# Recurrent stage: where the preparation of the next unit stands on PE, ACT and DVE

## The chip, the cores and the metric

The kernel runs on one core of a Trainium2 chip, as one program with a queue of instructions for each engine: PE (matrix products), ACT (activations and copies), DVE (elementwise work), POOL and SP. The metric is the time of one execution on the device, in microseconds (us), and lower is better.

## What is computed

Two transformer layers run after each other. The change touches one stage of the second: the bidirectional RWKV-7 scan of `rwkv7_time_mix`, cut here to its core (512 tokens, 8 heads of 64, both directions).

```python
w_raw = w0 + einsum('btr,drc->dbtc', tanh(wl), w2)          # low-rank product 1
decay = exp(-exp(-softplus(-w_raw) - 0.5))                   # = exp(-k * sigmoid(w_raw))
a = sigmoid(a0 + einsum('btr,drc->dbtc', al, a2))            # low-rank product 2
kk = k * k_k; kk = kk / maximum(sqrt(sum(kk * kk)), 1e-12)   # unit keys
k_dir = k * (1 + (a - 1) * k_a)
def step(state, inp):                                        # per head and direction
    r_t, w_t, k_t, v_t, a_t, b_t = inp                       # a_t = -kk, b_t = kk * a
    sa = einsum('dbhij,dbhj->dbhi', state, a_t)
    state = state * w_t[..., None, :] + sa[..., :, None] * b_t[..., None, :] + v_t[..., :, None] * k_t[..., None, :]
    return state, einsum('dbhij,dbhj->dbhi', state, r_t)
```

## The kernel before

`rwkv_block` computes the scan by chunks of 64 tokens. The work is cut into eight units: unit u is one tile of 128 features (two heads, `fi = u // 2`) in one direction (`d = u % 2`); "even" units go forwards, "odd" ones backwards. Each engine runs a list of instructions that is written out by hand, in order, and they meet at semaphores. A unit has these steps.

- **Attention** (`attention(u)`): PE makes five groups of 64x64 products of the scaled operands `a_s, b_s, k_s, r_s`, called m0 to m4 below, into PSUM (`bank`); before, ACT has set `x_t` and `x` to the identity (`r_masks`); DVE masks the groups into `ab_t`, `rk_t`, `rb_t`, `ak_t` and puts the first level into `x_t` and `x`.
- **Doubling**, levels k = 1 to 5 (`double(u, k)`): the inverse of a unit triangular matrix. At each level PE multiplies `x` by `ab_t` for both heads, ACT copies the result to `z` (two copies), PE makes the products of `x_t` and `z` (four groups; at level 5 two, of one kind), and DVE writes each into `x` or `x_t` under a mask (`copy_predicated`, four; at level 5 two). After level 1 PE also makes `keys_values(u)` (`ak_t` by `v_tm`), which ACT copies to `wr`.
- **Late part** (`late(u)`): products of `x_t` and `wr`, the transposes of the next unit's operands (`turn(u + 1)`), then long runs of 64x64 products that end the unit.

The **preparation of unit u + 1** is laced into the doubling of unit u: on PE `lora_products` (the two low-rank products, after level 1), on ACT `rates` (two sigmoids into `sg` and `rate`) and `decays` (three exponentials), each behind a load of ACT's table; on DVE `unit_keys` (maximum, reciprocal and product over `rw_t`, once for two units), `sums` (a scan and one or two sums into `cum` and `before`), `directed` (`kdir`, `rate`) and `scale` (six operations which write `a_s, b_s, k_s, r_s`). The order on DVE is

```python
if k == 1 and u % 2: unit_keys(u // 2 + 1)
elif k == 2:         sums(u + 1)
elif k == 3:         directed(u + 1)
elif k == 4:         scale(u + 1)
```

PSUM banks 6 and 7 are shared in turn by the low-rank products, the transposes and `keys_values`: the nth user (`side(n)`) waits until user n - 2 has been read (`side_read`), and n is counted (`SIDE * u + ...`, seven for a unit).

Of the kernel before, what the change touches and what calls it, by code (L numbers as in the profile page):

```python
# [21 lines left out]
P = 128  # L22
# [1855 lines left out]
def rwkv_block(nc, io, C, PV, zr, rw_t):  # L1878
# [6 lines left out]
    with ExitStack() as ctx:  # L1885
# [63 lines left out]
        hp = lambda hh: slice(64 * hh, 64 * hh + 64)  # L1949
        level = lambda side, k: four(levels[:, side, k, :])  # L1950
        R_, K_, V_ = 0, RW_FI, 2 * RW_FI
        SIDE, PR = 7, 18
        W = NB * CH
        NZ = 2 * (LEVELS - 1)

# [17 lines left out]
        def _(pe):  # L1973
# [5 lines left out]

            def lora_products(u):  # L1980
                fi, d = unit(u)
                nc.tensor.matmul(side(SIDE * u), lora[0:64, d, fi * P:fi * P + P], zr[0:64, 12, :], start=True, stop=True).then_inc(side_done, 1)
                nc.tensor.matmul(side(SIDE * u + 1), lora[64:128, d, fi * P:fi * P + P], zr[64:128, 12, :], start=True, stop=True).then_inc(side_done, 1)

            def turn(u):
                fi, d = unit(u)
                pe.wait_ge(tt_done, 4 * (u + 1))
                for k, src in enumerate((a_s[:, d], b_s[:, d], k_s[:, d], zr[:, V_ + fi, :])[0:4 - d]):
                    out = side(SIDE * u + 2 + k)
                    for t in range(NB):  # L1990
                        last = nc.tensor.transpose(tile(out, t), tile(src, t), C("ident"))
                    last.then_inc(side_done, 1)
                if d == 1:
                    out = side(SIDE * u + 5)
                    nc.tensor.matmul(out, C("head_ones"), bz[:, 0, :], start=True, stop=False)
                    nc.tensor.matmul(out, C("head_ones"), bz[:, 1, :], start=False, stop=True).then_inc(side_done, 1)

# [48 lines left out]
            def keys_values(u):  # L2046

                fi, d = unit(u)
                out = side(SIDE * u + 6)
                for hh in range(2):  # L2050
                    last = block_products(lambda half, t: out[hp(half), (hh * NB + t) * HD:(hh * NB + t) * HD + HD],
                                          lambda half, t: ak_t[hp(half), hh, t, :],
                                          lambda half, t: v_tm[hp(half), fi % 2, t, hh * HD:hh * HD + HD])
                last.then_inc(side_done, 1)

            def late(u):
                fi, d = unit(u)
                pe.wait_ge(side_read, SIDE * (u + 1))
                for hh in range(2):
                    pe.wait_ge(cp_done, PR * (u + 1) - 1 + hh)  # L2060
                    block_products(lambda half, t: bank[hp(half), 2 + hh, t * P:t * P + P], lambda half, t: x_t[hp(half), hh, t, :],
# [44 lines left out]
            lora_products(0)  # L2106
            turn(0)
            for u in range(NU):
                attention(u)
                for k in range(1, LEVELS):  # L2110
                    double(u, k)
                    if k == 1:
                        keys_values(u)
                        if u + 1 < NU:
                            lora_products(u + 1)
                late(u)

            pe.wait_ge(y0_read, NU)
# [40 lines left out]
        def _(act):  # L2159
            def rates(u):  # L2160

                fi, d = unit(u)
                if u:
                    act.wait_ge(tt_done, 4 * u)
                act.wait_ge(side_done, SIDE * u + 1)
                nc.scalar.activation(sg[:], bank[:, 6 + SIDE * u % 2, :], ACT.Sigmoid, bias=column("w0", 4 * d + fi)).then_inc(side_read, 1)
                act.wait_ge(side_done, SIDE * u + 2)
                nc.scalar.activation(rate[:], bank[:, 7 - SIDE * u % 2, :], ACT.Sigmoid, bias=column("a0", 4 * d + fi)).then_inc(side_read, 1)

            def decays(u):  # L2170
                act.wait_ge(c_done, u + 1)
# [3 lines left out]

            def token_major(u):
                fi, d = unit(u)
                n = SIDE * u
                act.wait_ge(levels_done, 1)
                act.wait_ge(side_done, n + 3)  # L2180
                nc.scalar.activation(wr[:, d, :, :, 0:HD].rearrange("p h t f -> p t h f"),
                                     bank[:, 6 + n % 2, :].rearrange("p (t h f) -> p t h f", t=NB, h=2), ACT.Copy).then_inc(side_read, 1)
                last = (v_tm[:, fi % 2].rearrange("p a b -> p (a b)") if d == 0 else bz[:, 0, :])
                for k, dst in ((3, b_tm[:, d].rearrange("p a b -> p (a b)")), (4, k_tm[:, d].rearrange("p a b -> p (a b)")), (5, last)):
                    act.wait_ge(side_done, n + k + 1)
                    nc.scalar.activation(dst, bank[:, 6 + (n + k) % 2, :], ACT.Copy).then_inc(side_read, 1)

            def keys_values(u):
                n = SIDE * u + 6
# [27 lines left out]
            for u in range(NU):  # L2217
                if u:
                    act.wait_ge(wu_done, 2 * u)
                else:  # L2220
                    act.wait_ge(masks_loaded, 16)
                for dst in (x_t, x):
                    nc.scalar.activation(blocks(dst[:]), eight(mask("ident")), ACT.Copy).then_inc(x_init, 1)
                for k in range(1, LEVELS):
                    for hh in range(2):
                        act.wait_ge(z_done, NZ * u + 2 * (k - 1) + hh + 1)
                        nc.scalar.activation(z[:, hh].rearrange("p a b -> p (a b)"), bank[:, 4 + hh, 0:W], ACT.Copy).then_inc(z_read, 1)
                    if k == 1:
                        keys_values(u)
                    if u + 1 < NU:  # L2230
                        if k == 1:
                            rates(u + 1)
                        elif k == 3:
                            decays(u + 1)
                late(u)
            for t in range(NB):
                act.wait_ge(centred, t + 1)
# [13 lines left out]
        def _(dve):  # L2251
            def sums(u):

                fi, d = unit(u)
                dve.wait_ge(side_read, SIDE * u + 1)
# [12 lines left out]
            def directed(u):  # L2268

                fi, d = unit(u)  # L2270
                dve.wait_ge(side_read, SIDE * u + 2)
# [19 lines left out]

            def bonus(u):
                fi, d = unit(u)
                dve.wait_ge(side_read, SIDE * u + 6)
# [49 lines left out]
            a0 = PARAMS["k_a"][0]  # L2344
            nc.vector.tensor_scalar(ka1[:], PV[:, a0:a0 + RW_FI], -1.0, 1.0, ALU.mult, ALU.add).then_inc(ka1_done, 1)
            dve.wait_ge(ka1_done, 1)
            def unit_keys(fi):

                dve.wait_ge(kstd, fi + 1)
                nc.vector.tensor_scalar(rw_t[:, fi, :], rw_t[:, fi, :], 1e-12, None, ALU.max).then_inc(kmax, 1)  # L2350
                dve.wait_ge(kmax, fi + 1)
                nc.vector.reciprocal(rw_t[:, fi, :], rw_t[:, fi, :]).then_inc(krec, 1)
                dve.wait_ge(krec, fi + 1)
                nc.vector.scalar_tensor_tensor(rw_t[:, fi, :], zr[:, K_ + fi, :], column("k_k", fi), rw_t[:, fi, :],
                                               ALU.mult, ALU.mult).then_inc(kk_done, 1)
            unit_keys(0)
            dve.wait_ge(levels_loaded, 16)
            nc.vector.tensor_copy(levels[:].rearrange("p a b c -> p (a b c)"), level_in).then_inc(levels_done, 1)
# [3 lines left out]
            for u in range(NU):  # L2362
                attention(u)
                for k in range(1, LEVELS):
# [4 lines left out]
                        dve.wait_ge(pr_done, pr_at(u, k, hh, 1))  # L2369
                        nc.vector.copy_predicated(x_t[:, hh], level(1 - u % 2, k), tiles64(bank[:, hh, 0:W])).then_inc(cp_done, 1)  # L2370
                    if u + 1 < NU:
                        if k == 1 and u % 2:
                            unit_keys(u // 2 + 1)
                        elif k == 2:
                            sums(u + 1)
                        elif k == 3:
                            directed(u + 1)
                        elif k == 4:
                            scale(u + 1)
                late(u)  # L2380
            dve.wait_ge(d_read, NU)
            dve.wait_ge(g_read, NU)
# [428 lines left out]
```

## Time and profile before

| | |
|---|---|
| median of 3 runs | 2093.97 us (2093.49 to 2095.81) |
| profiled execution | 2093.16 us, of which span 2091.4 us |
| PE busy | 1807.6 us (86%) |
| DVE busy | 1025.6 us (49%) |
| ACT busy | 729.7 us (35%) |
| attention of unit 0 to the end of unit 7 | from 1225.56 us to about 1502 us of the span |

The span is the time between the first and the last instruction that the profiler recorded; the profiled execution's own time has 1.8 us around it. Busy shares are means over stages with different limits, so that they say little about this stage; it is read by its own timeline.

### The profile page before, as it was taken

What the parts mean: (1) busy time and instruction counts of PE and PEld (TensorE: products, weight loads), DVE (VectorE), ACT (ScalarE), POOL (GpSimd) and SP (SyncE); (2) the same over time, 40 slices, a digit from 0 to 9 for tenths busy, and PEclk for the clock granted to TensorE, in tenths of its full rate; (3) what the DMA queues carried; (4) which work ended last, traced back from release to release, by engine and by line L of the source; (5) the groups of instructions that cost most, each with busy time, mean ns of one, the idle gap of its engine ahead of it and who ended that gap; (6) DMA issues with size and microseconds to landing.
All of it is one profiled execution on the core that took longest, in us unless ns stands there. A gap on an engine that the chain in (4) does not pass through costs nothing. (4 is left out here: it accounts for less than half of the span.)

```text
span 2091.4 us, 37559 instructions
## 1 busy us (share of the span) xinstructions
PE 1807.6 (86%) x16504; PEld 1542.5 (74%) x16504; DVE 1025.6 (49%) x1500; ACT 729.7 (35%) x1193; POOL 112.9 (5%) x133
## 2 busy tenths in 40 slices
PE   6999889838999999639999868888859899999988
PEld 5898768838989989438677657777738688878867
DVE  4145554456534635536454256756565544343445
ACT  3332234414434424223333253434233332232322
POOL 6000000030000000300000000000000200000020
PEclk9999979868999999769999989999979899999999
DMA  5211120102222222022122000000042122222221
GB/s 156 87 55 45 63 81 1 42 17 105 100 87 96 83 98 90 12 96 81 63 89 94 38 23 4 3 4 3 8 171 99 63 101 82 100 101 97 85 81 61
DMA packets 29256, 144.49 MB, mean 69 GB/s; under 512 B 6315, under 2 KB 9659, under 8 KB 14508
## 3 DMA queue, kind: packets, MB, share of 16 engines
q1 hardware_dynamic: 25116, 134.10, 17.9%
q0 software_dynamic: 3696, 7.35, 1.2%
q8 instruction: 126, 2.06, 0.4%
q10 hardware_dynamic: 288, 0.73, 0.1%
q14 instruction: 30, 0.25, 0.0%
HBM read 134.82 MB, written 8.91 MB: 69 GB/s over the span
## 5 line engine op out<-in xcount | busy, mean ns | idle before, releaser
L240 PE MATMUL f_bank<-f_u_hi,f_w_hi 128*128 128x258 f32 x704 | 201.1, 286 | 18.7 <-DVE f_w_lo L228 17.0
L241 PE MATMUL f_bank<-f_u_hi,f_w_lo 128*128 128x258 f32 x704 | 200.7, 285 | 0.0
L242 PE MATMUL f_bank<-f_u_lo,f_w_hi 128*128 128x258 f32 x704 | 199.1, 283 | 0.0
L240 PE MATMUL g_bank<-g_u_hi,g_w_hi 128*128 128x512 f32 x384 | 152.9, 398 | 17.0 <-DVE g_u_lo L2624 13.6
L241 PE MATMUL g_bank<-g_u_hi,g_w_lo 128*128 128x512 f32 x384 | 151.4, 394 | 0.0
L242 PE MATMUL g_bank<-g_u_lo,g_w_hi 128*128 128x512 f32 x384 | 151.2, 394 | 0.0
L240 PE MATMUL g_bank<-g_y_hi,g_w_hi 128*128 128x512 f32 x336 | 133.1, 396 | 18.5 <-DVE g_w_lo L228 11.7
L240 PEld LDWEIGHTS f_bank<-f_u_hi,f_w_hi 128*128 128x128 f32 x704 | 133.4, 190 | 20.3 <-DVE f_w_lo L228 17.8
L215 ACT ACTIVATE g_w_hi<-g_w_raw 128x2048 fp32r<-128x2048 f32 x45 | 85.9, 1909 | 174.4 <-PE g_bank L242 172.0
L242 PEld LDWEIGHTS f_bank<-f_u_lo,f_w_hi 128*128 128x128 f32 x704 | 134.4, 191 | 0.0
L241 PEld LDWEIGHTS f_bank<-f_u_hi,f_w_lo 128*128 128x128 f32 x704 | 133.8, 190 | 0.0
L241 PE MATMUL g_bank<-g_y_hi,g_w_lo 128*128 128x512 f32 x336 | 132.5, 394 | 0.0
L242 PE MATMUL g_bank<-g_y_lo,g_w_hi 128*128 128x512 f32 x336 | 132.3, 394 | 0.0
L228 DVE TENSOR_TENSOR g_w_lo<-g_w_raw,g_w_hi 128x2048 fp32r<-128x2048 f32 x45 | 103.2, 2292 | 48.5 <-ACT g_w_hi L215 48.3
L240 PEld LDWEIGHTS g_bank<-g_u_hi,g_w_hi 128*128 128x128 f32 x384 | 73.0, 190 | 39.5 <-issue 20.0
L228 DVE TENSOR_TENSOR f_w_lo<-f_w_raw,f_w_hi 128x2048 fp32r<-128x2048 f32 x34 | 77.9, 2292 | 47.8 <-ACT f_w_hi L215 47.7
L1606 PE MATMUL a_bank<-a_u_hi,a_w_hi 128*128 128x512 f32 x240 | 98.6, 411 | 1.3 <-ACT a_qkv L1705 0.6
L1610 PE MATMUL a_bank<-a_u_lo,a_w_hi 128*128 128x512 f32 x240 | 98.3, 409 | 0.0
L1608 PE MATMUL a_bank<-a_u_hi,a_w_lo 128*128 128x512 f32 x240 | 98.0, 408 | 0.0
L240 PEld LDWEIGHTS g_bank<-g_y_hi,g_w_hi 128*128 128x128 f32 x336 | 64.1, 191 | 34.6 <-issue 17.0
L242 PEld LDWEIGHTS g_bank<-g_u_lo,g_w_hi 128*128 128x128 f32 x384 | 73.3, 191 | 15.7
L2634 DVE TENSOR_TENSOR h<-g_bank,h 128x512 f32<-128x512 f32 x40 | 27.7, 691 | 114.8 <-PE g_bank L242 114.8
(445 smaller groups left out, 4319.1 us busy)
## 6 DMA issues: line engine op xcount, KB each, us to landing
g_w_raw<-in_w_ff SPq DMA_DIRECT2D x32, 1024.0 KB, 4.8
f_w_raw<-in_w_ffn_in SPq DMA_DIRECT2D x22, 1024.0 KB, 4.8
a_w_raw<-in_w_in SPq DMA_DIRECT2D x18, 1024.0 KB, 4.9
m_w_raw<-in_w_in SPq DMA_DIRECT2D x12, 1024.0 KB, 4.8
f_w_raw<-in_w_ffn_out SPq DMA_DIRECT2D x12, 1024.0 KB, 4.8
m_w_raw<-in_w_o SPq DMA_DIRECT2D x4, 1024.0 KB, 5.1
gate_pre<-rw_t POOLq DMA_DIRECT2D x16, 256.0 KB, 2.3
g_w_raw<-in_w_up SPq DMA_DIRECT2D x4, 1024.0 KB, 8.8
```

The lines of the kernel that those rows point to most:

```text
L215: nc.scalar.activation(R.hi[:, r, 0:size], R.raw[:, r, 0:size], ACT.Copy).then_inc(R.hi_done, 1)
L228: nc.vector.tensor_tensor(R.lo[:, r, 0:size], R.raw[:, r, 0:size], R.hi[:, r, 0:size].bitcast(F32), ALU.subtract).then_inc(R.split, 1)
L240: nc.tensor.matmul(out, w_hi, u_hi, start=start, stop=False)
L241: nc.tensor.matmul(out, w_lo, u_hi, start=False, stop=False)
L242: return nc.tensor.matmul(out, w_hi, u_lo, start=False, stop=stop)
L1606: nc.tensor.matmul(tile_bank(g), w_hi, u_hi[:, k, :], start=k == 0, stop=False)
L1608: nc.tensor.matmul(tile_bank(g), w_lo, u_hi[:, k, :], start=False, stop=False)
L1610: last = nc.tensor.matmul(tile_bank(g), w_hi, u_lo[:, k, :], start=False, stop=k == KT - 1)
L2634: nc.vector.tensor_tensor(x[:, t, :], bank[:, (2 * r + m) % 4, :], x[:, t, :], ALU.add).then_inc(R.tile_free, 1)
```

## The change

`lora_products(u + 1)` now stands ahead of `attention(u)` on PE, `rates(u + 1)` ahead of the doubling on ACT, right behind the two identity copies, and `decays(u + 1)` behind level 2. On DVE `sums`, `directed` and `scale` stand one level lower (1, 2, 3 for 2, 3, 4), and the reciprocal of the unit keys is cut into four tiles of 128 columns, done at levels 2 to 5 of the even unit ahead (`lengths` at level 1), so that only one product of it is left at level 1 of the odd unit. The counting of the users of banks 6 and 7 follows the new order (`lora_at`, `turn_at`, `keys_at`). No product and no element of the work is added or left out.

```diff
-        SIDE, PR = 7, 18
+        PR = 18
+        lora_at = lambda u: 7 * u - 1 if u else 0
+        turn_at = lambda u: 7 * u + 2
+        keys_at = lambda u: 7 * u + (8 if u + 1 < NU else 6)
...
             def late(u):
                 fi, d = unit(u)
-                pe.wait_ge(side_read, SIDE * (u + 1))
+                pe.wait_ge(side_read, keys_at(u) + 1)
...
             for u in range(NU):
+                if u + 1 < NU:
+                    lora_products(u + 1)
                 attention(u)
                 for k in range(1, LEVELS):
                     double(u, k)
                     if k == 1:
                         keys_values(u)
-                        if u + 1 < NU:
-                            lora_products(u + 1)
                 late(u)
...
                 for dst in (x_t, x):
                     nc.scalar.activation(blocks(dst[:]), eight(mask("ident")), ACT.Copy).then_inc(x_init, 1)
+                if u + 1 < NU:
+                    rates(u + 1)
                 for k in range(1, LEVELS):
...
                     if k == 1:
                         keys_values(u)
-                    if u + 1 < NU:
-                        if k == 1:
-                            rates(u + 1)
-                        elif k == 3:
-                            decays(u + 1)
+                    if k == 2 and u + 1 < NU:
+                        decays(u + 1)
                 late(u)
...
-            def unit_keys(fi):
-
+            def lengths(fi):
                 dve.wait_ge(kstd, fi + 1)
                 nc.vector.tensor_scalar(rw_t[:, fi, :], rw_t[:, fi, :], 1e-12, None, ALU.max).then_inc(kmax, 1)
+
+            def inverse_lengths(fi, t):
                 dve.wait_ge(kmax, fi + 1)
-                nc.vector.reciprocal(rw_t[:, fi, :], rw_t[:, fi, :]).then_inc(krec, 1)
-                dve.wait_ge(krec, fi + 1)
+                nc.vector.reciprocal(tile(rw_t[:, fi, :], t), tile(rw_t[:, fi, :], t)).then_inc(krec, 1)
+
+            def unit_keys(fi):
+                dve.wait_ge(krec, NB * (fi + 1))
...
                     if u + 1 < NU:
-                        if k == 1 and u % 2:
-                            unit_keys(u // 2 + 1)
+                        if k == 1:
+                            sums(u + 1)
+                            if u % 2:
+                                unit_keys(u // 2 + 1)
                         elif k == 2:
-                            sums(u + 1)
+                            directed(u + 1)
                         elif k == 3:
-                            directed(u + 1)
-                        elif k == 4:
                             scale(u + 1)
+                    if u % 2 == 0 and u + 2 < NU:
+                        if k == 1:
+                            lengths(u // 2 + 1)
+                        else:
+                            inverse_lengths(u // 2 + 1, k - 2)
                 late(u)
```

On PE, from the transposes ahead of unit 0 to the end of its level 1, these rows stood before:

```order
L1991 MATMUL r_bank<-consts,zr 128x128 x4
L2013 MATMUL r_bank<-r_a_s,r_b_s 64x64 x16
L2013 MATMUL r_bank<-r_b_s,r_a_s 64x64 x16
L2013 MATMUL r_bank<-r_r_s,r_k_s 64x64 x16
L2013 MATMUL r_bank<-r_r_s,r_b_s 64x64 x16
L2013 MATMUL r_bank<-r_a_s,r_k_s 64x64 x16
```

and behind level 1 of the doubling:

```order
L2021 MATMUL r_bank<-r_v_tm,r_ak_t 64x64 x16
L1982 MATMUL r_bank<-zr,r_lora 128x512
L1983 MATMUL r_bank<-zr,r_lora 128x512
L2021 MATMUL r_bank<-r_x,r_ab_t 64x64 x16
L2021 MATMUL r_bank<-r_z,r_x_t 64x64 x8
```

Now, in the same two places (three lines of the file further down):

```order
L1994 MATMUL r_bank<-consts,zr 128x128 x4
L1985 MATMUL r_bank<-zr,r_lora 128x512
L1986 MATMUL r_bank<-zr,r_lora 128x512
L2016 MATMUL r_bank<-r_a_s,r_b_s 64x64 x16
L2016 MATMUL r_bank<-r_b_s,r_a_s 64x64 x16
```

```order
L2024 MATMUL r_bank<-r_v_tm,r_ak_t 64x64 x16
L2024 MATMUL r_bank<-r_x,r_ab_t 64x64 x16
L2024 MATMUL r_bank<-r_z,r_x_t 64x64 x8
L2024 MATMUL r_bank<-r_x_t,r_z 64x64 x8
L2024 MATMUL r_bank<-r_z,r_x_t 64x64 x8
```

The two low-rank products (`r_lora`) have left the place between `keys_values` (`r_ak_t`) and level 2, and stand ahead of m0.

On DVE, in unit 0 (an even one), from the four masked copies of level 4 to the two of level 5, before:

```order
L2368 COPY_PREDICATED r_x<-r_levels,r_bank 128x256
L2370 COPY_PREDICATED r_x_t<-r_levels,r_bank 128x256
L2368 COPY_PREDICATED r_x<-r_levels,r_bank 128x256
L2370 COPY_PREDICATED r_x_t<-r_levels,r_bank 128x256
L2284 SCALAR_TENSOR_TENSOR r_bz<-r_kdir,params,zr 128x512
L2286 COPY r_pc<-r_cum 128x8
L2287 SCALAR_TENSOR_TENSOR r_a_s<-rw_t,r_before 128x512
L2288 TENSOR_TENSOR r_b_s<-r_rate,r_e_neg 128x512
L2289 TENSOR_TENSOR r_k_s<-r_kdir,r_e_neg 128x512
L2290 TENSOR_TENSOR r_r_s<-zr,r_cum 128x512
L2370 COPY_PREDICATED r_x_t<-r_levels,r_bank 128x256 x2
```

and now, from the second operation of `scale` (it follows the copies of level 3) to those of level 5:

```order
L2289 COPY r_pc<-r_cum 128x8
L2290 SCALAR_TENSOR_TENSOR r_a_s<-rw_t,r_before 128x512
L2291 TENSOR_TENSOR r_b_s<-r_rate,r_e_neg 128x512
L2292 TENSOR_TENSOR r_k_s<-r_kdir,r_e_neg 128x512
L2293 TENSOR_TENSOR r_r_s<-zr,r_cum 128x512
L2356 RECIPROCAL rw_t<-rw_t 128x128
L2377 COPY_PREDICATED r_x<-r_levels,r_bank 128x256
L2379 COPY_PREDICATED r_x_t<-r_levels,r_bank 128x256
L2377 COPY_PREDICATED r_x<-r_levels,r_bank 128x256
L2379 COPY_PREDICATED r_x_t<-r_levels,r_bank 128x256
L2356 RECIPROCAL rw_t<-rw_t 128x128
L2379 COPY_PREDICATED r_x_t<-r_levels,r_bank 128x256 x2
```

`scale` has moved from ahead of level 5's copies to ahead of level 4's, with a tile of the reciprocal behind it, and ahead of level 5 only such a tile is left (in odd units, nothing).

On ACT, from the identity copies to level 3 of the same unit, before:

```order
L2223 ACTIVATE r_x_t<-r_masks 128x512
L2223 ACTIVATE r_x<-r_masks 128x512
L2227 ACTIVATE r_z<-r_bank 128x256 x2
L2191 ACTIVATE r_wr<-r_bank 128x8x64
L2166 ACT_TABLE_LOAD
L2166 ACTIVATE r_sg<-r_bank,params 128x512
L2168 ACTIVATE r_rate<-r_bank,params 128x512
L2227 ACTIVATE r_z<-r_bank 128x256 x4
L2172 ACT_TABLE_LOAD
```

and now:

```order
L2227 ACTIVATE r_x_t<-r_masks 128x512
L2227 ACTIVATE r_x<-r_masks 128x512
L2170 ACT_TABLE_LOAD
L2170 ACTIVATE r_sg<-r_bank,params 128x512
L2172 ACTIVATE r_rate<-r_bank,params 128x512
L2233 ACTIVATE r_z<-r_bank 128x256 x2
L2195 ACTIVATE r_wr<-r_bank 128x8x64
L2233 ACTIVATE r_z<-r_bank 128x256 x2
L2176 ACT_TABLE_LOAD
```

The load and the two sigmoids have moved ahead of level 1's copies to `z`; the second load, with the exponentials, has moved from behind level 3's to behind level 2's.

## Rows read from the trace of the kernel before

**Rows 1.** Busy time in unit 1: start and end, length, engines, granted clock (PEclk), DMA share.

```profile
1260.85:1295.50 34.65, 29.18 (x894) 25.45 (x888) 24.23 (x41) 14.49 (x27) 0.00 (x0) 1.00 0.02 4
```

**Rows 2.** Waits of PE in 1225 to 1500 us: total us, times, longest.

```profile
PE r_bank L2021 <- DVE r_x_t L2370: 14.8, 11, 1.7
PE r_bank L2013 <- issue: 9.1, 9, 1.8
```

**Rows 3.** Timeline of PE in unit 1: start, length, what [idle before <- releaser].

```profile
1260.85 0.68 PE L2013 MATMUL r_bank<-r_a_s,r_b_s 64*64 64x64 f32 x32
...
1264.01 0.50 PE L2013 MATMUL r_bank<-r_r_s,r_b_s 64*64 64x64 f32 x17 [0.84 <-issue]
...
1265.97 0.68 PE L2021 MATMUL r_bank<-r_z,r_x_t 64*64 64x64 f32 x16
...
1269.63 1.12 PE L1982 MATMUL r_bank<-zr,r_lora 64*128 64x512 f32 x2
...
1271.44 1.15 PE L2021 MATMUL r_bank<-r_x,r_ab_t 64*64 64x64 f32 x32
1273.72 0.68 PE L2021 MATMUL r_bank<-r_z,r_x_t 64*64 64x64 f32 x16 [1.13 <-ACT r_z L2227]
...
1275.63 1.39 PE L2021 MATMUL r_bank<-r_x,r_ab_t 64*64 64x64 f32 x32
1276.86 0.63 PE L2021 MATMUL r_bank<-r_z,r_x_t 64*64 64x64 f32 x16
...
1280.76 0.68 PE L2021 MATMUL r_bank<-r_z,r_x_t 64*64 64x64 f32 x16 [0.45 <-ACT r_z L2227]
...
1283.90 1.33 PE L2021 MATMUL r_bank<-r_x_t,r_z 64*64 64x64 f32 x32
1286.95 1.96 PE L2021 MATMUL r_bank<-r_wr,r_x_t 64*64 64x128 f32 x32 [1.72 <-DVE r_x_t L2370]
```

**Rows 4.** Timeline of ACT in unit 1.

```profile
1270.83 1.28 ACT L2166 ACT_TABLE_LOAD   x1 [0.50 <-PE r_bank L1982]
1272.13 0.69 ACT L2166 ACTIVATE r_sg<-r_bank,params 128x512 f32<-128x512 f32 x1
...
1273.28 0.66 ACT L2227 ACTIVATE r_z<-r_bank 128x256 f32<-128x256 f32 x2
...
1277.47 1.28 ACT L2172 ACT_TABLE_LOAD   x1
...
1280.34 0.64 ACT L2227 ACTIVATE r_z<-r_bank 128x256 f32<-128x256 f32 x2
```

**Rows 5.** Timeline of DVE in unit 1.

```profile
1262.80 0.69 DVE L2304 TENSOR_TENSOR r_ab_t<-r_bank,r_masks 128x512 f32<-128x512 f32 x1 [2.34 <-ACT r_x L2223]
...
1274.45 0.45 DVE L2368 COPY_PREDICATED r_x<-r_levels,r_bank 128x256 f32<-128x256 uint8 x1 [0.71 <-PE r_bank L2021]
...
1276.28 1.23 DVE L2258 TENSOR_TENSOR_SCAN r_cum<-r_reset,r_sg 128x512 f32<-128x512 f32 x1
...
1278.15 0.44 DVE L2368 COPY_PREDICATED r_x<-r_levels,r_bank 128x256 f32<-128x256 uint8 x1
...
1279.47 0.54 DVE L2273 TENSOR_SCALAR r_kdir<-r_rate,params,r_ka 128x512 f32<-128x512 f32 x1
...
1280.66 0.69 DVE L2276 TENSOR_TENSOR r_rate<-r_rate,rw_t 128x512 f32<-128x512 f32 x1
...
1283.23 0.74 DVE L2284 SCALAR_TENSOR_TENSOR r_bz<-r_kdir,params,zr 128x512 f32<-128x512 f32 x1
...
1286.38 0.77 DVE L2370 COPY_PREDICATED r_x_t<-r_levels,r_bank 128x256 f32<-128x256 uint8 x2
```

**Rows 6.** Reciprocals of DVE by shape: busy us, mean ns of one.

```profile
L2352 DVE RECIPROCAL rw_t<-rw_t 128x512 f32<-128x512 f32 x4 | 13.4, 3353 | 0.1
L1853 DVE RECIPROCAL a_st<-a_st 128x1 f32<-128x1 f32 x32 | 4.9, 153 | 2.0 <-ACT a_s L1772 2.0
```

**Rows 7.** The product of wr in unit 3, from PE's timeline.

```profile
1357.84 3.30 PE L2021 MATMUL r_bank<-r_wr,r_x_t 64*64 64x128 f32 x32 [1.72 <-DVE r_x_t L2370]
```

More of the change, by code:

```diff
@@ L1981, in lora_products @@
                 fi, d = unit(u)
-                nc.tensor.matmul(side(SIDE * u), lora[0:64, d, fi * P:fi * P + P], zr[0:64, 12, :], start=True, stop=True).then_inc(side_done, 1)
-                nc.tensor.matmul(side(SIDE * u + 1), lora[64:128, d, fi * P:fi * P + P], zr[64:128, 12, :], start=True, stop=True).then_inc(side_done, 1)
+                nc.tensor.matmul(side(lora_at(u)), lora[0:64, d, fi * P:fi * P + P], zr[0:64, 12, :], start=True, stop=True).then_inc(side_done, 1)
+                nc.tensor.matmul(side(lora_at(u) + 1), lora[64:128, d, fi * P:fi * P + P], zr[64:128, 12, :], start=True, stop=True).then_inc(side_done, 1)
             def turn(u):
@@ L1988, in turn @@
                 for k, src in enumerate((a_s[:, d], b_s[:, d], k_s[:, d], zr[:, V_ + fi, :])[0:4 - d]):
-                    out = side(SIDE * u + 2 + k)
+                    out = side(turn_at(u) + k)
                     for t in range(NB):
@@ L1993, in turn @@
                 if d == 1:
-                    out = side(SIDE * u + 5)
+                    out = side(turn_at(u) + 3)
                     nc.tensor.matmul(out, C("head_ones"), bz[:, 0, :], start=True, stop=False)
@@ L2048, in keys_values @@
                 fi, d = unit(u)
-                out = side(SIDE * u + 6)
+                out = side(keys_at(u))
                 for hh in range(2):
@@ L2164, in rates @@
                     act.wait_ge(tt_done, 4 * u)
[L2165 to L2168, printed above, removed]
+                n = lora_at(u)
+                act.wait_ge(side_done, n + 1)
+                nc.scalar.activation(sg[:], bank[:, 6 + n % 2, :], ACT.Sigmoid, bias=column("w0", 4 * d + fi)).then_inc(side_read, 1)
+                act.wait_ge(side_done, n + 2)
+                nc.scalar.activation(rate[:], bank[:, 7 - n % 2, :], ACT.Sigmoid, bias=column("a0", 4 * d + fi)).then_inc(side_read, 1)
             def decays(u):
@@ L2177, in token_major @@
                 fi, d = unit(u)
-                n = SIDE * u
+                n = turn_at(u)
                 act.wait_ge(levels_done, 1)
-                act.wait_ge(side_done, n + 3)
+                act.wait_ge(side_done, n + 1)
                 nc.scalar.activation(wr[:, d, :, :, 0:HD].rearrange("p h t f -> p t h f"),
@@ L2183, in token_major @@
                 last = (v_tm[:, fi % 2].rearrange("p a b -> p (a b)") if d == 0 else bz[:, 0, :])
-                for k, dst in ((3, b_tm[:, d].rearrange("p a b -> p (a b)")), (4, k_tm[:, d].rearrange("p a b -> p (a b)")), (5, last)):
+                for k, dst in ((1, b_tm[:, d].rearrange("p a b -> p (a b)")), (2, k_tm[:, d].rearrange("p a b -> p (a b)")), (3, last)):
                     act.wait_ge(side_done, n + k + 1)
@@ L2188, in keys_values @@
             def keys_values(u):
-                n = SIDE * u + 6
+                n = keys_at(u)
                 act.wait_ge(side_done, n + 1)
@@ L2254, in sums @@
                 fi, d = unit(u)
-                dve.wait_ge(side_read, SIDE * u + 1)
+                dve.wait_ge(side_read, lora_at(u) + 1)
                 if u:
@@ L2270, in directed @@
                 fi, d = unit(u)
-                dve.wait_ge(side_read, SIDE * u + 2)
+                dve.wait_ge(side_read, lora_at(u) + 2)
                 dve.wait_ge(kk_done, fi + 1)
@@ L2293, in bonus @@
                 fi, d = unit(u)
-                dve.wait_ge(side_read, SIDE * u + 6)
+                dve.wait_ge(side_read, turn_at(u) + 4)
                 nc.vector.tensor_tensor(rw_t[:, fi, :], bz[:, 0, :], zr[:, V_ + fi, :], ALU.mult).then_inc(bonus_done, 1)
@@ L2346, in _ @@
             dve.wait_ge(ka1_done, 1)
-            def unit_keys(fi):
+            def lengths(fi):
                 dve.wait_ge(kstd, fi + 1)
                 nc.vector.tensor_scalar(rw_t[:, fi, :], rw_t[:, fi, :], 1e-12, None, ALU.max).then_inc(kmax, 1)
+            def inverse_lengths(fi, t):
                 dve.wait_ge(kmax, fi + 1)
-                nc.vector.reciprocal(rw_t[:, fi, :], rw_t[:, fi, :]).then_inc(krec, 1)
-                dve.wait_ge(krec, fi + 1)
+                nc.vector.reciprocal(tile(rw_t[:, fi, :], t), tile(rw_t[:, fi, :], t)).then_inc(krec, 1)
+            def unit_keys(fi):
+                dve.wait_ge(krec, NB * (fi + 1))
                 nc.vector.scalar_tensor_tensor(rw_t[:, fi, :], zr[:, K_ + fi, :], column("k_k", fi), rw_t[:, fi, :],
                                                ALU.mult, ALU.mult).then_inc(kk_done, 1)
+            lengths(0)
+            for t in range(NB):
+                inverse_lengths(0, t)
             unit_keys(0)
```

## The prediction

> **What bounds the kernel now.** I looked first at the busy time of the stretches, to see whether an engine fills the recurrent stage. None does: in unit 1, 34.65 us long, PE is busy for 29.2 us, DVE for 24.2 and ACT for 14.5, at the full granted clock of 1.00, and transfers are at a share of 0.02 [rows 1]. So the stage is a chain that runs from engine to engine, and a gain lies where one waits for another. The list of PE's waits is to be read for who ends them: 14.8 us for DVE's masked copies into `x_t`, in 11 waits, and 9.1 us of "issue", in which PE waited for nothing that the profile shows, 9 times, at most 1.8 us [rows 2]. The timelines of unit 1 then show where they lie [rows 3 to 5]. I measure a level by P1 to P5, the starts of PE's products of `z` and `x_t`: 1265.97, 1273.72, 1276.86, 1280.76 and 1283.90, and W, the start of the products of `wr`, at 1286.95 [rows 3]. P1 to W takes 20.98 us. A level where nothing disturbs takes 3.14 (P2 to P3, P4 to P5). The others are longer for three reasons. P1 to P2 takes 7.75: the low-rank products hold PE for 1.81 us (1269.63 to 1271.44), and then the copies to `z` stand on ACT behind a table load and two sigmoids, so that PE waits 1.13 us [rows 3, 4]. P3 to P4 takes 3.90: ACT's load and exponentials last from 1277.47 to 1280.34, and `z` comes behind them [rows 3, 4]. P5 to W takes 3.05: DVE works on `scale` from 1283.23 to 1286.38, with level 5's two copies behind it, and PE waits 1.72 us [rows 3, 5].
>
> **The start of a unit.** PE now issues 1.81 us of low-rank products ahead of m0. In unit 1 m0 moves from 1260.85 to 1262.66, and with its 0.68 us ends at 1263.34; DVE, which began its first mask at 1262.80, released by ACT's identity copy, begins at 1263.4 [rows 3, 5]. The cost is 0.6 us. It is not 1.81, because PE was ahead of the chain there: behind its groups lay a gap of 0.84 us on "issue" [rows 3]. Such gaps come about once in a unit, 1.0 us in the mean [rows 2], behind the longest stretch in which PE issues without a pause. I take them as the sequencer falling behind, and expect that 1.81 us with only two products to issue lets it catch up. If a gap stays whole, PE and not DVE ends the start and the cost is 0.8 more. Where the gap was longest, the chain was held by it already, and the cost is nearer nothing; I take 0.3 as the mean of units 1 to 6, with 0 and 1.1 as bounds. Unit 0 has ACT's copies of the transposes ahead of the products (banks 6 and 7 must be read first): between 0.6 and 1.8, taken as 1.0. Unit 7 prepares nothing and does not change.
>
> On the page "Runtime: NRT & Kernel Launch", section "Instruction fetch mechanics", the Trainium skill says that PE's instructions are fetched in 16 KiB blocks and that the fetch is mostly hidden. By that rule there would be no such gaps to absorb and none to fear; the trace disagrees, with 9.1 us of them.
>
> On ACT, load and sigmoids last 1.30 and 1.15 us (1270.83, 1272.13, 1273.28) [rows 4]. Behind the identity copy they run from 1262.8 to 1265.25. Level 1's first copy to `z` is wanted 0.4 us ahead of P1 (the copy at 1280.34 gave products at 1280.76), thus at 1266.1 with the shift. So they cost nothing, with 0.85 us of cover; DVE's masks and PE's groups are what hides them.
>
> On the page "ScalarE: Activation LUTs", section "What ACT_TABLE_LOAD costs", the Trainium skill adds a drain of about 1380 ns to each load of 1283 ns. Here the sigmoid starts 0.02 us behind the load's end. By the page it would be 0.5 us late for `z` in seven units, some 4 us in all; the row speaks against it.
>
> **P1 to P2.** From P1 to the old place of the low-rank products is 3.66 us; level 2's first product now starts there, and undisturbed it stands 1.2 us ahead of the products (1275.63 to 1276.86) [rows 3]. That is 4.86 for 7.75. DVE has `sums` there (1.87 us, 1276.28 to 1278.15; one more sum of some 0.7 for an odd next unit), and 0.7 of unit keys or 0.4 of `lengths`: up to 3.0 us [rows 5]. It fills most of the 4.86; I estimate level 2's copies at most half a us late, which they make up since ready copies run faster (below).
>
> **P2 to P3.** The exponentials come here: 3.8 for 3.14, by the same 2.87 us on ACT. DVE has `directed`, 1.8 us (1279.47 to 1281.3); it is free at P2 + 2.56 (1276.28) and done at P2 + 4.4, when the first copy is wanted 0.73 behind P3, at P2 + 4.5 [rows 3, 5]. In even units a tile of the reciprocal follows. Its form is not in the trace. The bounds are a quarter of 3353 ns, 0.84, and that plus the 0.15 of a single column, 0.99 [rows 6]; I take 0.9. It makes the copies 0.75 late.
>
> **P3 to P4.** Free of exponentials: 3.14 for 3.90 in odd units. DVE catches up in part, since copies that are ready run at 0.33 us (four from 1278.15 to 1279.47). From the first late copy to the next products there are 2.1 us: three copies, 0.57 to PE's start (1286.38 to 1286.95), and half a group of `x` by `ab_t` [rows 3, 5]. For even units that gives 3.6.
>
> **P4 to P5** takes the stall. `scale` (3.15 us) starts at P3 + 2.56 and ends at P4 + 2.6; plus 2.1, P5 is P4 + 4.7 in place of 3.14. In even units, with the tile and the lateness, it is 5.4. **P5 to W** has only a tile or nothing: copy wanted at 0.73, PE 0.57 later, 1.3 for 3.05.
>
> **The sum.** Odd units, and unit 6, which has no later keys: 4.86 + 3.8 + 3.14 + 4.7 + 1.3 = 17.8 for 20.98, a gain of 3.2. Units 0, 2 and 4: 4.86 + 3.8 + 3.6 + 5.4 + 1.3 = 19.0, a gain of 2.0. Four of the one and three of the other make 18.8. Off go 1.8 for the starts of units 1 to 6, 1.0 for unit 0, and 0.3 for the four tiles in place of one reciprocal ahead of unit 0, where DVE is the chain (four times the 0.15 of a single column is 0.6, no overhead is 0). That leaves 15.7: 2093.16 - 15.7 = 2077.5 for the profiled execution, which stood 0.8 below the median of the runs, so 2078.
>
> **The rivals.**
> - The gaps stay whole. For: they follow a count of instructions, which the move hardly changes. Against: the two products are time without issue. 0.8 us in six units, 5 us: 2083.
> - DVE or ACT is somewhat later than worked out: the copies keep the 0.47 us spacing that they have under PE's products, half a us in each of seven units, or the drain is real. 3.5 to 4 us: 2082. Nothing in the rows asks for it.
> - The idle time at level 4 (some 1.4 us in odd units, 2.2 in even ones) lowers PE's clock. In unit 3, behind a wait of 1.72 us, the products of `wr` took 3.30 us for 1.96 [rows 3, 7]. One such drop costs 1.3 us. As many as before change nothing, one in each unit costs 7 more: 2085.
> - Slower than before: the same idle time of even units drops the clock and leaves it at half for the following dense part of 12 us, W to the next m3 (1286.95 to some 1299). At the ratio 3.30 to 1.96 that is 8 us a unit. From two such units on the gain is gone; four make it slower, 2093.
> - Better: gaps gone with no cost at the start, and no clock drop (2 in the old stage would be 2.6): 2072.
> - The change does nothing, the wait only moves: P4 to P5 would have to take 3 us more still. DVE would have to be the bound, and its 24.2 us of 34.65 leave room.
>
> **How the numbers follow.** My forecast, 2075 to 2080, has 0.50; the gaps 0.16; the later DVE or ACT 0.12; clock drops 0.08; better 0.08; nothing 0.04; slower 0.02. 2071 to 2086 holds all but the last two and a tail. Within 0.2%, 4.2 us, is about what a measurement of this kernel can't tell from no change: faster 0.93, same 0.04, slower 0.03.
>
> **What would show it.** P1 to P2 near 4.9 us with no wait for `r_z`; the wait of 1.72 ahead of `r_wr` gone; a new wait of 1.4 to 2.2 us for DVE ahead of level 5, longer in even units; the first mask of a unit about 0.6 later behind m0; the "issue" gaps at m3 smaller. It is wrong if gaps stand at m3 in full, if `z` waits for sigmoids at level 1, or if the granted clock of the units falls.

## The result and the profile after

The changed kernel takes 2070.28 us (median of 4 runs, 2067.5 to 2072.68) against 2094.89 us before (4 runs, 2093.49 to 2096.68): a ratio of 0.9882, 95% interval 0.9864 to 0.9899, 24.6 us faster. In five more runs it took 2070.01 us, against 2092.35 us in ten of before: 0.9894 (0.9878 to 0.9911). The forecast was 2078 us, with a range of 2071 to 2086: right in sign, but the gain was half as much again as the 16 us forecast, and the time lies 0.7 us below the range.

First the busy time of unit 1 of the changed kernel, from the start of the last product of unit 0 to that of unit 1 (columns as in [rows 1]):

```profile
1261.23:1292.42 31.19, 28.16 (x896) 25.14 (x889) 20.31 (x39) 14.61 (x27) 0.00 (x0) 1.00 0.02 4
```

PE has the same work in 31.2 us that had 34.65 [rows 1]. PE's waits in the stage, 1225 to 1500 us:

```profile
PE r_bank L2024 <- DVE r_x_t L2379: 12.2, 10, 2.0
PE r_bank L2016 <- issue: 5.9, 7, 1.5
PE r_bank L2024 <- ACT r_z L2233: 1.5, 4, 0.4
```

The wait for DVE fell little, to 12.2 us from the 14.8 of [rows 2]; the waits on issue fell to 5.9 from 9.1, but don't vanish. PE's timeline of unit 1, beside [rows 3]:

```profile
1261.38 0.69 PE L1985 MATMUL r_bank<-zr,r_lora 64*128 64x512 f32 x1
1261.39 0.69 PE L1986 MATMUL r_bank<-zr,r_lora 64*128 64x512 f32 x1
...
1262.44 0.69 PE L2016 MATMUL r_bank<-r_a_s,r_b_s 64*64 64x64 f32 x32
...
1264.67 0.51 PE L2016 MATMUL r_bank<-r_r_s,r_b_s 64*64 64x64 f32 x19 [0.39 <-issue]
...
1266.64 0.68 PE L2024 MATMUL r_bank<-r_z,r_x_t 64*64 64x64 f32 x16
...
1271.03 0.68 PE L2024 MATMUL r_bank<-r_z,r_x_t 64*64 64x64 f32 x16
...
1274.73 0.68 PE L2024 MATMUL r_bank<-r_z,r_x_t 64*64 64x64 f32 x16 [0.39 <-ACT r_z L2233]
...
1277.87 0.63 PE L2024 MATMUL r_bank<-r_z,r_x_t 64*64 64x64 f32 x16
...
1281.16 1.34 PE L2024 MATMUL r_bank<-r_x,r_ab_t 64*64 64x64 f32 x32 [1.26 <-DVE r_x_t L2379]
1282.34 1.33 PE L2024 MATMUL r_bank<-r_x_t,r_z 64*64 64x64 f32 x32
1283.64 1.96 PE L2024 MATMUL r_bank<-r_wr,r_x_t 64*64 64x128 f32 x32
```

P1 to P5 and W are 1266.64, 1271.03, 1274.73, 1277.87, 1282.34 and 1283.64: steps of 4.39, 3.70, 3.14, 4.47 and 1.30 where 7.75, 3.14, 3.90, 3.14 and 3.05 stood. The wait of 1.72 us ahead of `r_wr` is gone, and a wait of 1.26 us for DVE stands ahead of level 5. The two low-rank products start within 0.01 us of each other, and m0 follows 1.06 us later, not 1.81.

ACT and DVE in the same unit, beside [rows 4] and [rows 5]:

```profile
1263.17 1.28 ACT L2170 ACT_TABLE_LOAD   x1
1264.46 0.69 ACT L2170 ACTIVATE r_sg<-r_bank,params 128x512 f32<-128x512 f32 x1
...
1266.20 0.85 ACT L2233 ACTIVATE r_z<-r_bank 128x256 f32<-128x256 f32 x2 [0.47 <-PE r_bank L2024]
```

```profile
1263.30 0.69 DVE L2307 TENSOR_TENSOR r_ab_t<-r_bank,r_masks 128x512 f32<-128x512 f32 x1 [2.76 <-PE r_bank L2016]
...
1277.20 0.75 DVE L2287 SCALAR_TENSOR_TENSOR r_bz<-r_kdir,params,zr 128x512 f32<-128x512 f32 x1
...
1280.34 0.43 DVE L2377 COPY_PREDICATED r_x<-r_levels,r_bank 128x256 f32<-128x256 uint8 x1
```

The sigmoids end 0.47 us before `z` is wanted, so they are hidden. `scale` runs from 1277.20 to 1280.34 with level 4's copies behind it: the stall that stood ahead of W now stands ahead of level 5. A tile of the reciprocal took 0.94 us (beside the 3353 ns of [rows 6]):

```profile
L2356 DVE RECIPROCAL rw_t<-rw_t 128x128 f32<-128x128 f32 x16 | 14.7, 936 | 0.0
```

The parts of the stage, in us, as sums over the units, measured between the starts of the same instructions; the end of a unit is the start of its last product. Two profiles of before and three of the changed kernel are averaged; a spread is given where it exceeds 0.5. "Forecast" and "measured" are gains.

| part | before | changed | forecast | measured |
|---|---|---|---|---|
| P1 to P2, units 0 to 6 | 51.8 | 30.6 (30.0 to 31.1) | 20.2 | 21.2 |
| P2 to P3 | 22.0 | 25.9 | -4.6 | -3.9 |
| P3 to P4 | 27.8 | 23.4 | 3.9 | 4.4 |
| P4 to P5 | 22.0 | 34.2 (33.7 to 34.8) | -13.0 | -12.2 |
| P5 to W | 21.4 | 9.6 (9.1 to 9.9) | 12.3 | 11.7 |
| end of a unit to P1 of the next, units 1 to 7 | 38.8 | 38.9 (37.9 to 39.8) | -1.8 | 0 |
| first transpose to P1, unit 0 | 8.4 | 10.7 (9.3 to 11.4) | -1.0 | -2.3 |
| W to the end, units 0 to 7 | 73.7 | 71.5 (70.8 to 72.5) | 0 | 2.2 |
| sum, first transpose to end of unit 7 | 280.5 | 259.5 (259.2 to 260.1) | 16.0 | 21.0 |

### The profile page after: what moved, and what is told of

It is laid out like the page before. It is cut to its first block and busy times, and to the rows that moved or that the text cites. A ratio compares the mean times of both kernels' runs of the same rounds, so it can differ in the third digit from the quotient of the medians.

```text
span 2070.9 us, 37571 instructions
## 1 busy us (share of the span) xinstructions
PE 1801.4 (87%) x16504; PEld 1538.2 (74%) x16504; DVE 1024.6 (49%) x1512; ACT 730.8 (35%) x1193; POOL 113.0 (5%) x133
```

## The experiments

**The changed kernel once more.** No edit.

> The changed kernel once more, in more rounds, to tell a real distance from the scatter of runs. Theory A (the levels of the doubling gained 21.5 us and the rest is the granted clock, which falls at varying places): the steps of the stage repeat to 0.1 us per level, the median lies within 2068 to 2073, and what differs between profiles is where the clock is at half and the gaps on issue. Theory B (the first sample was a lucky one): the median comes out at 2074 or more.

2070.01 us (2067.55 to 2072.12). Where no clock drop fell, the steps from P2 to W repeated to 0.02 us; P1 to P2, in which gaps on issue fall, differed by up to 0.6 us in a unit. The first transpose of unit 0 came at 1219.7 us of the span, for 1221.7 in the first profile. Over all fourteen profiles of this case it came between 1217.5 and 1223.3, though no edit lies ahead of the stage and its prologue; from the end of unit 7 to the end of the span it took 587.5 to 590.0 us, and the stage of the changed kernel 259.2 to 260.1 in three profiles. So the profiles of one kernel differ mostly by what lies ahead of the stage; why that part varies is open. Theory A holds for the steps and the median, but it looked for the scatter in the stage, where the least of it is.

**Low-rank products one after the other.**

```diff
+                pe.wait_ge(side_done, lora_at(u) + 1)
                 nc.tensor.matmul(side(lora_at(u) + 1), lora[64:128, d, fi * P:fi * P + P], zr[64:128, 12, :], start=True, stop=True).then_inc(side_done, 1)
```

> The changed kernel, with the second low-rank product waiting for the end of the first. In the changed kernel the two ran at the same time, 1.06 us for both; in the kernel before one after the other, 1.81. Theory A (they ran in sequence before only because the second one's bank had to be read by ACT, and this side by side running made the start of a unit cheaper than forecast): the start of each of six units costs 0.75 us more, 4 to 5 us slower than the changed kernel. Theory B (PE's gaps on issue take it up): the gaps at m3 shrink by as much, and it is at most 1.5 us slower.

2079.16 us (2077.74 to 2081.36), 9 us slower than the changed kernel on the same chip; the stage took 267.9 us for 259.5. PE's timeline at unit 1:

```profile
1259.47 1.12 PE L1985 MATMUL r_bank<-zr,r_lora 64*128 64x512 f32 x2
1260.65 1.12 PE L1987 MATMUL r_bank<-zr,r_lora 64*128 64x512 f32 x2
1261.70 0.69 PE L2017 MATMUL r_bank<-r_a_s,r_b_s 64*64 64x64 f32 x32
...
1263.97 0.52 PE L2017 MATMUL r_bank<-r_r_s,r_b_s 64*64 64x64 f32 x20 [0.49 <-issue]
```

The products now take 2.23 us (1259.47 to 1261.70) for 1.06. Before the change it was 1.81, since the second started 0.76 us behind the first; here it starts 1.18 us behind, so that 0.12 us are for the wait itself. The way from the end of a unit to P1 rose from 38.9 to 46.6 in all, 1.3 for each of six units, and the waits on issue stayed (5.6 us). For this further time PE is the bound at the start of a unit, and Theory B falls. Theory A's mechanism holds; its size was too small, because it priced the second product at the old 0.75 and not at 1.18.

**Scale back behind level 4.**

```diff
-                        elif k == 3:
+                        elif k == 4:
                             scale(u + 1)
```

> The changed kernel with scale back behind level 4, all else as changed. Theory A (the gain is made at P1 to P2, and the stall of scale is only moved): P4 to P5 3.14 and P5 to W 3.05 in odd units, 4.0 in even ones, in place of 4.47 + 1.30 and 5.27 + 1.30; in all 3 us slower than the changed kernel. Theory B (bringing scale down from level 4 is what pays, since it frees PE ahead of wr): 10 to 12 us slower.

2075.62 us (2072.16 to 2085.11), 5.6 slower; the stage took 263.3 us, 3.8 more. The steps came as A said: P4 to P5 3.09 to 3.13, P5 to W 3.05 in odd units and unit 6 (which has no reciprocal to do) and 3.86 in units 0, 2 and 4, 1.7 us more in all. Behind W lie 5.4 us more, and P1 to P2 and the starts of the units took 3 us less than in the mean of the changed kernel's profiles:

```profile
1313.31 3.48 PE L2024 MATMUL r_bank<-r_wr,r_x_t 64*64 64x128 f32 x32 [2.53 <-DVE r_x_t L2379]
```

Behind the wait of 2.53 us the products of `wr` took 3.48 us for 1.96: the granted clock was at half (1.2 of 2.4 GHz). It was in three units of seven, and W to the end rose from 71.5 to 76.9. The profile is that of the fastest of the five runs, so that its 3.8 us may be too few. Theory A holds in the levels, and Theory B falls: bringing `scale` down is worth 4 to 6 us on top of the rest, most of it by the clock, and not 10 to 12.

**Only the early products and sigmoids.** PE and the sigmoids as changed; on DVE the order of before, the exponentials behind level 3.

```diff
-                    if k == 2 and u + 1 < NU:
+                    if k == 3 and u + 1 < NU:
                         decays(u + 1)
...
                         if k == 1:
-                            sums(u + 1)
                             if u % 2:
+                                lengths(u // 2 + 1)
+                                for t in range(NB):
+                                    inverse_lengths(u // 2 + 1, t)
                                 unit_keys(u // 2 + 1)
                         elif k == 2:
+                            sums(u + 1)
+                        elif k == 3:
                             directed(u + 1)
-                        elif k == 3:
+                        elif k == 4:
                             scale(u + 1)
```

> Only the first part of the change: low-rank products ahead of m0 and sigmoids behind the identity copies; on DVE the order of before (sums, directed, scale at levels 2, 3, 4, the whole reciprocal at level 1 of odd units), decays behind level 3. Theory A (the early low-rank products give the time between P1 and P2, but in odd units the whole reciprocal then stands in the way on DVE): P1 to P2 4.4 in all units, P2 to P3 3.1 in even and 5.5 in odd units, then 3.9 to 4.0, 3.14, 3.05; 7 to 10 us faster than before. Theory B (the early products give all of the gain): 20 us faster than before.

2080.24 us (2078.5 to 2083.59), 12 us faster than the 2092.35 of before and 10 slower than the changed kernel. P1 to P2 was 30.5 in all, as in the changed kernel; P2 to P3 3.1 in even and 5.03 in odd units. Theory A holds in its steps (for the odd units 5.5 was forecast), and the gain is a little more than its 7 to 10 us. So the time between P1 and P2 can be had without the lower levels, but the whole reciprocal takes some of it back in odd units.

**The whole reciprocal at level 1 of odd units**, all else as changed.

```diff
+                            if u % 2:
+                                lengths(u // 2 + 1)
+                                for t in range(NB):
+                                    inverse_lengths(u // 2 + 1, t)
                                 unit_keys(u // 2 + 1)
```

> The changed kernel with the whole reciprocal (four tiles one after the other, as they are) at level 1 of odd units, as before the change. Theory A (cutting it up and spreading it over the even unit is what lets the early sums pay in odd units): level 2's copies come 4 us late, P2 to P3 7 us for 3.7 in units 1, 3 and 5, while even units gain 1.3 each; 5 to 7 us slower than the changed kernel. Theory B (it would be hidden at level 1, as it was before the change): 3 to 4 us faster, from the even units.

2078.42 us (2076.27 to 2080.69), ratio to before 0.9922 (0.9901 to 0.9942). The changed kernel ran in another series; by the ratios to before (0.9882 and 0.9894 there) this one is 6 to 8 us slower. DVE's timeline of unit 1:

```profile
1269.41 3.39 DVE L2356 RECIPROCAL rw_t<-rw_t 128x128 f32<-128x128 f32 x4
1272.83 0.75 DVE L2360 SCALAR_TENSOR_TENSOR rw_t<-zr,params,rw_t 128x512 f32<-128x512 f32 x1
1273.50 0.43 DVE L2377 COPY_PREDICATED r_x<-r_levels,r_bank 128x256 f32<-128x256 uint8 x1
```

P2 to P3 was 7.46 in units 1, 3 and 5, as A said, and the half clock lay behind each of these waits, which made P3 to P4 4.7 to 4.85 for 3.14. One after the other the four tiles took 3.39 us, 0.04 longer than the whole (3353 ns, [rows 6]): cutting it up costs next to nothing. In one piece it holds up the copies of level 2; spreading it out is one way around that, and the next run shows a better one.

**The reciprocal in the late part.**

```diff
-                    if u % 2 == 0 and u + 2 < NU:
-                        if k == 1:
-                            lengths(u // 2 + 1)
-                        else:
-                            inverse_lengths(u // 2 + 1, k - 2)
+                if u % 2 == 0 and u + 2 < NU:
+                    lengths(u // 2 + 1)
+                    for t in range(NB):
+                        inverse_lengths(u // 2 + 1, t)
                 late(u)
```

> The changed kernel, with the maximum and the four tiles of the reciprocal behind level 5 of even units, where DVE stood idle for 5 to 6 us until the bonus. Theory A (the tiles at levels 2 to 4 of even units lie on the chain): in units 0, 2 and 4 P3 to P4 3.14 for 3.62, P4 to P5 4.47 for 5.3; about 4 us faster than the changed kernel. Theory B (they are hidden, or the bonus comes later by as much): no difference beyond 1 us.

2065.05 us (2061.03 to 2065.94), 5 us below the changed kernel, which ran in another series (the stage took 254.6 us for 259.5); ratio to before 0.9856 (0.9835 to 0.9877). All of units 0 to 6 now had 3.14 and 4.47. Theory A.

**Scale in two parts.** `r_bz`, `pc` and `a_s` behind level 3, the other three behind level 4 (`scale_rest`).

```diff
                         elif k == 3:
                             scale(u + 1)
+                        elif k == 4:
+                            scale_rest(u + 1)
```

> The changed kernel, with scale cut in two: r_bz, pc and a_s behind level 3, b_s, k_s and r_s behind level 4. Theory A (a level takes about 1.2 us of other DVE work at no cost, and the rest goes on the chain one for one): in odd units P4 to P5 3.2 and P5 to W 1.8 in place of 4.47 and 1.30, in even ones 3.55 and 2.5 in place of 5.3 and 1.3; 5 us faster than the changed kernel. Theory B (the stall is only divided): no difference beyond 1 us.

2064.56 us (2059.53 to 2067.18), of which 252.9 for the stage; ratio to before 0.9852 (0.9829 to 0.9875). P4 to P5 was 3.09 and P5 to W 1.71 in odd units and unit 6, 3.47 and 2.52 in the other even ones: Theory A to 0.1 us.

**Both.**

> Both of these together. Theory A: all units 0 to 6 have P3 to P4 3.14, P4 to P5 3.2, P5 to W 1.8; 9 to 10 us faster than the changed kernel, about 2060 us. Theory B (the granted clock takes part of it back): the levels as by A, but less than 6 us faster, with the half clock inside the late parts.

2061.81 us (2056.32 to 2063.06), 0.9834 (0.9815 to 0.9854). P3 to W of unit 1, PE:

```profile
1273.80 0.68 PE L2024 MATMUL r_bank<-r_z,r_x_t 64*64 64x64 f32 x16 [0.39 <-ACT r_z L2233]
...
1276.94 0.63 PE L2024 MATMUL r_bank<-r_z,r_x_t 64*64 64x64 f32 x16
...
1280.03 1.33 PE L2024 MATMUL r_bank<-r_x_t,r_z 64*64 64x64 f32 x32
1281.74 1.96 PE L2024 MATMUL r_bank<-r_wr,r_x_t 64*64 64x128 f32 x32 [0.38 <-DVE r_x_t L2383]
```

P1 to W fell to 110.9 us from 123.7, and the stage to 248.2, 11.3 us less than in the changed kernel. Theory A holds for the levels; the medians differ by 8 us across two series, and no half clock lay in the levels or late parts, so that Theory B falls.

**Both once more, and with unit 0 started otherwise.**

> The kernel with the late reciprocal and the divided scale once more, beside the one in which unit 0 starts otherwise, so that the two are compared on the same chip. Theory A: 2060 to 2063 us, 7 to 10 us less than the changed kernel. Theory B (the first sample was lucky): 2064 or more.

2059.28 us (2050.09 to 2059.49), 0.9830 (0.9810 to 0.9850); stage 247.1 us. Theory A, and a little better. The other kernel has, beside these two edits,

```diff
                     last.then_inc(a_done, 1)
+                    if u == 0 and m == 2:
+                        lora_products(u + 1)
...
-                if u + 1 < NU:
+                if 0 < u < NU - 1:
                     lora_products(u + 1)
```

> The kernel with the late reciprocal and the divided scale, in which the low-rank products of unit 0 alone stand behind m2 of its attention, so that the first 64x64 products don't wait for them and for ACT's copies. In the changed kernel the way from the first transpose to P1 of unit 0 took 11.4 us in five profiles with a half clock of 17.1 us there, 9.3 to 9.9 in three with 10.2 us; in the kernel before 8.4. Theory A (the products ahead of m0 cost unit 0 1 us at full clock, and as much again by making the half clock last longer, since PE works less densely there): 8.5 to 9.5 us, half clock 10 us, 2 to 3 us faster than the kernel with both edits. Theory B (how long the half clock lasts here is chance): 0.5 to 1 us faster, half clock of either length.

2057.57 us (2056.7 to 2059.92), 0.9838 (0.9824 to 0.9851): not told apart from the kernel beside it. From the first transpose to P1 of unit 0 it took 9.17 us, and 9.25 in the kernel beside it, both with a half clock of 10.2 us. Theory A, a gain of 2 to 3 us, falls: PE no longer waited for the products, but in unit 0 it waited 0.73 us for `z` behind the sigmoids.

**Two more profiles.**

> The kernel before, once more, for its profile. Theory A: the steps of units 0 to 6 repeat within 1 us (P1 to W 144.7 in all); the half clock at unit 0 lasts 10 us again. Theory B (chance): it lasts 14 or 17 us, and the way from the first transpose to P1 of unit 0 takes up to 2 us more than 8.4.

> The changed kernel, a third profile. Theory A: P1 to W of units 0 to 6 between 123 and 124 us in all, half clock at unit 0 17 us again, 11.4 us from the first transpose to P1 of unit 0. Theory B (chance): a half clock of 10 us, 9.5 us.

Single times: 2089.3 us before, 2072.52 us changed. P1 to W was 145.1 us in all for before (144.7 in the first) and 123.8 for the changed kernel. The busy time at unit 0's start, 1212 to 1232 us, first in the changed kernel's first profile, then in its third (the clock is the third number from the end):

```profile
1212.00:1232.00 20.00, 10.31 (x182) 7.84 (x184) 11.64 (x19) 10.92 (x17) 0.00 (x0) 0.57 0.01 2
```

```profile
1212.00:1232.00 20.00, 10.26 (x256) 8.32 (x258) 13.29 (x23) 11.21 (x18) 0.00 (x0) 0.74 0.01 2
```

A mean clock of 0.57 is a half clock of 17.1 us, 0.74 one of 10.2. The same kernel showed both, with 11.4 and 9.3 us to P1. So for unit 0 chance (Theory B) holds: the products cost it 0.9 us, and up to 2.1 more hang on where the half clock ends. Whether the change makes the longer one more frequent stays open. Of the eleven profiles with low-rank products ahead of unit 0's m0 five had 17 us, one 13.6 and five 10; the two of before had 10, and so had the kernel with the products behind m2.

## Why the prediction was wrong

The chain, the moved stall and its new place came as forecast; the sum came out at 16.0 for the stage, with 0.3 off for the prologue, and measured 21.0. (The 0.3 was nearly nothing too: four tiles took 3.39 us ahead of unit 0, the whole 3.35.) Four terms were mis-sized, three of them the same way.

- **The start of a unit** (forecast 1.8 for units 1 to 6 and 0 for unit 7; measured 0.5, and a gain of 0.5 in unit 7). The step that failed is "PE now issues 1.81 us of low-rank products ahead of m0". The 1.81 belongs to the old place, not to the products. In the kernel before, PE and ACT had there:

```profile
1269.63 1.12 PE L1982 MATMUL r_bank<-zr,r_lora 64*128 64x512 f32 x2
1270.39 1.12 PE L1983 MATMUL r_bank<-zr,r_lora 64*128 64x512 f32 x2
```

```profile
1269.74 0.60 ACT L2191 ACTIVATE r_wr<-r_bank 128x512 f32<-128x512 f32 x1 [3.36 <-PE r_bank L2021]
```

  The second product's bank is the one that `keys_values` had filled, and it starts when ACT has read it (1270.34). Ahead of unit 0, where both banks were free, the same two ran side by side, and this row was in the trace before:

```profile
1209.37 0.69 PE L1982 MATMUL r_bank<-zr,r_lora 64*128 64x512 f32 x1
1209.37 0.69 PE L1983 MATMUL r_bank<-zr,r_lora 64*128 64x512 f32 x1
```

  They use rows 0 to 63 and 64 to 127 of the array. The serial kernel shows what that is worth: 1.3 us a unit. The Trainium skill, "TensorEngine Tiling (Array Packing)", section "Key Properties", says that tiles work independently and can run at once; the trace agrees.

  The other half of the step, that PE's gaps on issue absorb the products, was too hopeful, and the two errors cancel in part, by luck. In units 1 to 6 m0 came 1.16 us later behind the end of the unit before, and m0 to P1 took 4.32 us for 5.40, so that 1.08 were absorbed; 3.7 to 5.9 us of gaps stayed, for 9.1 and 9.5. The serial kernel pushed m0 back by 1.18 more, and m0 to P1 took 4.41: nothing more was absorbed. The forecast had 1.5 of 1.81 absorbed. Had the products taken 1.81 us, the start would by these figures have cost about 0.8 us a unit (an estimate), 5 us in all, which is what the rival "gaps stay whole" asked.
- **The levels** (18.8, measured 21.2). The shape was right throughout. The forecast had P1 to P2 at 4.86 where the mean was 4.37: it took P1 to the next level's first product as 3.66 from unit 1, which held a gap on issue of 0.32 us; the mean of seven units was 3.24. As it took 7.75 for the old step from the same unit, where the mean was 7.40, most of this cancels, and 1.0 us of gain is left over. P2 to P3 took 3.70 for 3.8 (0.7 us in all); P3 to P4 had taken 4.02 and not 3.90 in the even units of before (0.5); P4 to P5 took 4.47 for 4.7 and mostly 5.27 for 5.4 (0.8); P5 to W took 1.3 as forecast but for four units, in two of the three profiles, that had a half clock (0.5 the other way). In unit 7, which prepares nothing, DVE stood idle for 1.25 us between the copies of two levels; `scale`'s 3.14 less these 1.25, and less the 0.56 which four ready copies save at a spacing of 0.33 us for 0.47, is the 1.33 by which 4.47 exceeds 3.14.
- **The late parts** (0, measured 2.2). In both profiles of before, the products of `wr` ran at half clock in two units behind the wait of 1.72 us, at 3.1 to 3.6 us for 1.96 [rows 7], and such a late part took 1.5 to 1.6 us longer. The forecast let as many drops stand as before. As many did come in two of the three profiles of the changed kernel, two in each, and none in the first; but three of these four fell at level 5, behind the new wait of 2.0 us of even units, where one cost 1.0 us, and only one took the products of `wr` to 3.01. So the step that failed is "as many as before change nothing": a drop costs by where it falls. The rival "better" had no drop, for which 0.08 was given.
- **Unit 0** (1.0, measured 2.3) went the other way, by the length of the half clock.

The rest, 3.6 us of the 24.6, isn't found in the stage. The medians of 4 runs carry the scatter of what lies ahead of it, up to 6 us between profiles; the second series gave 22.3 us, and the five profiles 19.5 in the mean. The forecast knew three runs of before within 2.3 us and gave the range no term for it. With the table's 21.0 the forecast would have been 2073, inside its range, and 2070.28 within such a scatter; that the time fell outside is in part chance. The rivals: whole gaps did not come (that would be 9 us of them); neither later copies nor a drain behind the table load (the sigmoid starts 0.01 us behind the load's end at 1264.45); no clock drop held through a dense stretch.

**What the gaps on issue are.** The forecast took them "as the sequencer falling behind", and none of the experiments above asks why. The traces have more. Between 1225 and 1500 us of the kernel before, this line stands in the list of transfers (packets, MB, share):

```profile
q8 instruction: 54, 0.88, 1.3%
```

These are blocks of instructions, 16,384 bytes in a packet. In unit 1 one landed at 1262.71, the gap of 0.84 us ended at 1264.01, and the next block started at 1265.11. In all fourteen profiles together 158 gaps on issue of over 0.2 us lie in the stage up to 1485 us, and each ends 1.2 to 1.6 us behind the landing of such a block, though blocks follow each other at 4.1 us in the median and never at less than 3.2. So PE waits there for its next instructions, when it uses up a block faster than the next comes; no run varied this by itself. It fits that the two low-rank products, 1.06 us of work with few instructions, made the gaps behind them smaller.

## What to carry to other kernels

A duration between two rows belongs to the place as much as to the instructions: before moving an operation, look for the same one elsewhere in the trace where nothing holds it, and ask which semaphore its old spacing came from. In a chain in which PE, ACT and DVE take turns, a level that nothing else holds up has an allowance of foreign work (here some 1.2 us of DVE's); what exceeds it goes on the chain, but for what ready copies make up, so a long block should be cut to that size and spread, or put where its engine stands idle for longer. A sum of this kind should also take its base from the mean of all units and not from the one whose timeline is at hand.

## What the runs showed that was not expected

A wait of 1.7 us or more on PE can cost more than itself. In nine profiles the longest wait for DVE in the stage was 1.7 to 3.6 us, and in eight of them the clock behind unit 0's start fell to half (1.2 of 2.4 GHz) two or three times, for 3.4 or 6.8 us each; `wr`'s products then took up to 3.7 us for 1.96. In the five profiles in which no such wait was longer than 1.3 us (the late reciprocal, the divided `scale` and the kernels with both) it never did. The same wait of 1.72 us passed without a drop in five of seven units of the kernel before, while all three waits of 3.6 us in the kernel with the whole reciprocal brought one, so that it isn't the wait alone; what else it takes stays open. Two products that overlap in 1.06 us take 2.23 one after the other with a semaphore between them, of which the semaphore's part is 0.12. Four reciprocals of 128 columns took 3.39 us together, nearly the 3.35 of one of 512. And the program ahead of the stage, the same in all kernels, took 1217.5 to 1223.3 us in fourteen profiles.
